# Two-layer encoder with a mixture of experts on one core: query projections and local scores as three single-pass products, heads paired by key group, outputs split straight from PSUM, and an exit by quarters

## The reference, cut to what matters

```
h = RMSNorm(x);  z = h @ W_in -> c_q 384 | c_kv 256 | k_rope 32 | q_B 512 | k_B 128 | v_B 128 | g_A 1024 | g_B 1024
latent attention:  q = rms(c_q) @ W_uq (8 heads, 64 + 32 rotary), k, v from rms(c_kv) @ W_ukv and k_rope
                   softmax over all 256 keys, scale 96 ** -0.5
local attention:   8 heads of 64, 2 key heads (4 query heads each), |q - k| <= 128, relative bias, sink logit per head
x = x + (sigmoid(g_A) * (o_A @ W_oA) + sigmoid(g_B) * (o_B @ W_oB)) @ W_out
x = x + mixture of experts (32 experts, 2 per token) of RMSNorm(x)
```

## Time and profile before

| | |
|---|---|
| median of 3 runs | 1303.14 us |
| the profiled execution | 1301.5 us |
| its span | 1299.7 us |
| PE busy | 1245.8 us (96%) |
| DVE, ACT, POOL busy | 546.8, 415.2, 232.7 us |
| the chain of work that ended last | PE 88%, DVE 4%, DMA 3%, ACT 2% |
| granted TensorE clock, mean | 0.986 |

### The profile page before, as it was taken

How to read it: one execution, slowest core, us unless ns; L and a number is a source line. 1 busy time by engine, 2 the same in 40 slices (tenths; PEclk the granted TensorE clock), 3 DMA queues, 4 the chain that set the end, 5 groups by cost and what they waited for, 6 DMA issues and landing times.

```text
span 1299.7 us, 15960 instructions
## 1 busy us (share of the span) xinstructions
PE 1245.8 (96%) x5860; PEld 814.2 (63%) x5860; DVE 546.8 (42%) x837; ACT 415.2 (32%) x808; POOL 232.7 (18%) x246
## 2 busy tenths in 40 slices
PE   4999999999999999999999999899999899999996
PEld 4976567888874444444588666688888634444443
DVE  4447653342452233333463565434342513333335
ACT  4426663221222222222252467422221222222223
POOL 1343640000102111100324446100010111111000
PEclk9999999999998999999999999999999899999999
DMA  9503003334437999999913300133351599999991
GB/s 298 179 21 97 1 1 118 92 97 146 162 153 287 421 418 419 420 420 423 354 27 112 84 15 1 65 97 98 98 223 54 199 391 420 420 418 420 419 409 73
DMA packets 110521, 278.46 MB, mean 214 GB/s; under 512 B 12240, under 2 KB 74192, under 8 KB 102256
## 3 DMA queue, kind: packets, MB, share of 16 engines
q1 hardware_dynamic: 102752, 259.01, 52.2%
q0 software_dynamic: 6400, 13.74, 3.1%
q10 hardware_dynamic: 1296, 4.72, 0.9%
HBM read 279.52 MB, written 8.40 MB: 222 GB/s over the span
## 4 chain that ended last, share of the span: by engine, by line
PE 88%; DVE 4%; DMA 3%; ACT 2%; DVEq 1%; ACTq 1%; issue 1%; POOL 0%; SPq 0%
PE bank L1197 82%; PE bank L1463 2%; DMA ring<-w_gate_up 2%; PE bank L1332 2%; ACT arena L789 1%; DMA ring<-w_in 1%; DVE arena L873 1%; PE bank L1212 1%; DVE small L1023 1%; PE bank L1510 1%; ACTq L792 1%; PE bank L1395 0%; DVE small L1021 0%; PE bank L1257 0%; DVEq L1022 0%
## 5 line engine op out<-in xcount | busy, mean ns | idle before, releaser
L1197 PE MATMUL bank<-arena 128*64 128x512 f32 (+4 forms) x1410 | 319.2, 518 | 4.7 <-ACTq L755 1.9
L1197 PEld LDWEIGHTS bank<-arena 128*64 128x64 f32 (+2 forms) x1410 | 140.9, 151 | 157.2 <-issue 132.7
L1197 PE MATMUL bank<-ring,arena 128*64 128x512 f32 (+1 forms) x800 | 187.2, 599 | 0.8 <-DMA ring<-w_gate_up 0.4
L1197 PE MATMUL bank<-y_parts,chosen 128*128 128x512 f32 x512 | 134.0, 405 | 0.2
L1197 PEld LDWEIGHTS bank<-ring,arena 128*64 128x64 f32 (+1 forms) x800 | 59.9, 140 | 113.9 <-issue 112.3
L1143 DVE TENSOR_TENSOR x<-x,bank 128x512 f32<-128x512 f32 x128 | 88.0, 687 | 59.0 <-PE bank L1197 58.8
L1197 PEld LDWEIGHTS bank<-y_parts,chosen 128*128 128x128 f32 x512 | 91.2, 188 | 22.7 <-issue 3.5
L1197 PE MATMUL bank<-hT_gate_low,w_chunk_high 128*128 128x512 f32 x256 | 101.4, 396 | 2.1 <-DVE hT_gate_low L1037 2.1
L1197 PE MATMUL bank<-hT_gate_high,w_chunk_low 128*128 128x512 f32 x256 | 101.1, 395 | 0.0
L1197 PE MATMUL bank<-hT_gate_high,w_chunk_high 128*128 128x512 f32 x256 | 101.1, 395 | 0.0
L1164 DVE TENSOR_TENSOR arena<-arena,bank 128x256 f32<-128x256 f32 x32 | 13.5, 421 | 203.6 <-ACT arena L841 203.6
(11 more groups left out here) (205 smaller groups left out, 1917.2 us busy)
## 6 DMA issues: line engine op xcount, KB each, us to landing
ring<-w_gate_up SPq DMA_DIRECT2D x32, 2048.0 KB, 17.7
arena<-w_gate_up SPq DMA_DIRECT2D x32, 2048.0 KB, 18.2
ring<-w_down SPq DMA_DIRECT2D x32, 1024.0 KB, 16.8
arena<-w_down SPq DMA_DIRECT2D x32, 1024.0 KB, 17.8
ring<-w_in SPq DMA_DIRECT2D x36, 512.0 KB, 6.1
arena<-w_out SPq DMA_DIRECT2D x8, 1024.0 KB, 6.3
ring<-w_in SPq DMA_DIRECT2D x4, 1024.0 KB, 12.7
ring<-w_oa SPq DMA_DIRECT2D x16, 256.0 KB, 2.9
```

The costliest lines, as they stand in the source:

```text
L1197: return pe.matmul(out, lhsT, rhs, start=first, stop=last)
```

## The change

- **Queries:** `wq` and c_q (after the transposes) get a high and a low part; each query projection is `mm3` over three chunks. POOL builds `wk` first, then `wq` high (the same 24 instructions), then `wq` low: 12 subtractions and 12 small instructions more. c_q high is an ACT copy, c_q low a DVE subtraction out of PSUM. The parts take the place in the ring of column block 1's weights, so SP loads that block only after the last projection.
- **Local scores:** z tiles 8 to 12 are split by ACT (high) and DVE (low). The host permutes the head columns so that the pair in one tile has one head of each key group; a head's scores then take 64 rows of q and of k, as `mm3`, and `kz` with its zero halves goes.
- **Softmax:** the scale 96 ** -0.5 moves into the query copies and the rotary table; the maximum is written negated; the sink goes into its column by a maximum over one element, issued before the wait for the scores.
- **Outputs:** latent pairs get one rounded ACT copy; DVE subtracts straight from PSUM, in iterations 12, 14 and 16 and once after the loop, and the next output waits for it. hT_gate goes by quarters in the order of `GATE_K`. The first merge starts with the local half and waits for the last low part only before its last chunk.
- **cT** is made in the order 3, 4, 5, 0, 1, 2 in other banks.

The core of the diff:

```
-    rope_rows = np.concatenate([rows, rows], 1).astype(np.float32)
+    rope_rows = np.concatenate([rows, rows], 1).astype(np.float32) * np.float32(MLA_SCALE)
...
+        GATE_K = (6, 0, 2, 4)
+        LOW_AT = {4: 3, 5: 6, 6: 7}
...
# SP
+                    if j == 1:
+                        sp.wait_ge(proj_ps, l * 12 + 12)
+                        sp.nop(nofuse=True)
# POOL: kz fills removed; wk built here, before wq
+                    src, high, low_ = raw[:, :, e::2, :], wq_parts[0][:, :, e::2, :], wq_parts[1][:, :, e::2, :]
...
+                    pool.drain()
+                    for k in range(3):
+                        pool.tensor_tensor(low_[:, k, :, r0:r0 + 32], src[:, k, :, 64:96], high[:, k, :, r0:r0 + 32], ALU.subtract)
+                        pool.tensor_tensor(low_[:, k, :, n0:n0 + 64], src[:, k, :, 0:64], high[:, k, :, n0:n0 + 64], ALU.subtract)
+                    pool.drain()
+                    for k in range(3):
+                        pool.tensor_scalar(low_[:, k, :, r0 + 32:r0 + 48], low_[:, k, :, r0 + 16:r0 + 32], -1.0, None, ALU.mult)
+                        pool.tensor_copy(low_[:, k, :, r0 + 48:r0 + 64], low_[:, k, :, r0:r0 + 16])
# ACT
+                    if t >= 8:
+                        act.activation(z_split(t)[0], z_bank(t)[:, :], ACT.Copy).then_inc(z_high, 1)
+                        continue
...
+                act.wait_ge(cT_ps, l * 6 + 2)
+                act.activation(cT[:, 4, :], cT_bank(4)[:, :], ACT.Copy).then_inc(cT_act, 1)
+                for t in range(3):
+                    act.wait_ge(cT_ps, l * 6 + 4 + t)
+                    act.activation(cq_parts[0][:, t, :], cT_bank(t)[:, :], ACT.Copy).then_inc(cT_act, 1)
...
-                        act.activation(oT[:, 1 - m // 4, m % 4, :], bank[6][:, :], ACT.Copy)
-                        if m >= 4:
-                            act.activation(oT_high[0][m - 4], bank[6][:, :], ACT.Copy)
-                        act.drain().then_inc(oT_done, 1)
+                        act.activation(oT[:, 1, m, :] if m < 4 else oT_high[0][m - 4], bank[6][:, :], ACT.Copy).then_inc(oT_done, 1)
# DVE
+                    if t >= 8:
+                        dve.wait_ge(z_high, l * NZ_SPLIT + t - 7)
+                        dve.tensor_tensor(z_split(t)[1], z_bank(t)[:, :], z_split(t)[0], ALU.subtract).then_inc(z_low, 1)
...
+                for t in range(3):
+                    dve.wait_ge(cT_act, l * 4 + 2 + t)
+                    dve.tensor_tensor(cq_parts[1][:, t, :], cT_bank(t)[:, :], cq_parts[0][:, t, :], ALU.subtract).then_inc(cT_dve, 1)
...
+                        if n < H:
+                            dve.tensor_reduce(soft[:, n % 2, :, S:S + 1].rearrange("p c o -> p (c o)"),
+                                              sink_b[:, n:n + 1].unsqueeze(1).broadcast_to([P, C, 1]), AX.X, ALU.max)
+                        dve.wait_ge(scores_ps, l * HEADS + n + 1)
...
-                            dve.tensor_copy(soft[:, n % 2, :, S:S + 1].rearrange("p c o -> p (c o)"), sink_b[:, n:n + 1].broadcast_to([P, C]))
                             dve.drain()
-                            step(dve.tensor_reduce(mx, soft[:, n % 2, :, :], AX.X, ALU.max))
-                            dve.tensor_scalar(negmax[:, n % 2, :], mx, -1.0, None, ALU.mult).then_inc(negmax_ready, 1)
+                            dve.tensor_reduce(negmax[:, n % 2, :], soft[:, n % 2, :, :], AX.X, ALU.max, negate=True).then_inc(negmax_ready, 1)
...
-                            dve.drain()
-                            dve.tensor_scalar(negmax[:, n % 2, :], mx, -MLA_SCALE, None, ALU.mult).then_inc(negmax_ready, 1)
+                            peak.then_inc(negmax_ready, 1)
...
+                    for i in {HEADS - 2: (0,), HEADS - 1: (1,), HEADS: (2, 3)}.get(n, ()):
+                        dve.wait_ge(hT_gate_high, l * 4 + i + 1)
+                        dve.wait_ge(proj_ps, l * 12 + (12 if i else 10))
+                        k = slice(GATE_K[i], GATE_K[i] + 2)
                         dve.tensor_tensor(hT_gate[1][:, k, :], hT[:, k, :], hT_gate[0][:, k, :], ALU.subtract).then_inc(hT_gate_low, 1)
+                    if n in (12, 14, 16):
+                        low_output(n // 2 - 2)
+                low_output(7)
# PE
+                    if t == NZ_K:
+                        pe.wait_ge(z_low, l * NZ_SPLIT + 1)
+                for t in CT_ORDER:
+                    if t == 0:
+                        pe.wait_ge(z_low, l * NZ_SPLIT + 4)
...
+                pe.wait_ge(z_low, l * NZ_SPLIT + NZ_SPLIT)
...
-                            m = mm(bank[7][:, :], wq[:, k, 2 * j + kind - 1, :], cT[:, k, :], k == 0, k == 2)
+                            m = mm3(bank[7][:, :], [w[:, k, 2 * j + kind - 1, :] for w in wq_parts], [c[:, k, :] for c in cq_parts], k == 0, k == 2)
...
-                        if m_ >= 1:
+                        if 1 <= m_ <= 4:
                             pe.wait_ge(oT_done, l * H + m_)
+                        if m_ >= 5:
+                            pe.wait_ge(oT_low_ready, l * H + LOW_AT[m_ - 1])
...
+                                    rows = slice(n % 2 * HD, (n % 2 + 1) * HD)
+                                    q = qB_high[rows, n // 2, q0:q0 + P], qB_low[n // 2][rows, q0:q0 + P]
+                                    m = mm3(out, q, [k_[rows, b * S:(b + 1) * S] for k_ in kB], True, True)
...
-                        pe.wait_ge(oT_low_ready, l * H + H)
-                    for m in range(2):
+                        pe.wait_ge(oT_low_ready, l * H + H - 1)
+                    for m in (1, 0):
                         for k in range(4):
                             i = 4 * m + k
+                            if (j, m, k) == (0, 0, 3):
+                                pe.wait_ge(oT_low_ready, l * H + H)
```

More of the change, by code:

```diff
@@ L158, in encoder_kernel @@
         qBT_, qBT_at = take(4 * T)
-        kz_, _ = take(4 * T)
+        kz_, kz_at = take(4 * T)
         vB_, vB_at = take(C * P)
@@ L584, in _ @@
                 pool.nop(nofuse=True)
+                pool.wait_ge(ukv_in, l * 16 + 16)
+                pool.nop(nofuse=True)
+                raw_k = ukv_raw.rearrange("p k (h n) -> p k h n", h=H)
+                for k in range(2):
+                    pool.tensor_copy(wk[:, k, :].rearrange("p (h n) -> p h n", h=H), raw_k[:, k, :, 0:NOPE])
+                pool.drain().then_inc(wk_built, 1)
                 for e in range(2):
-                    src, dst = raw[:, :, e::2, :], wq[:, :, e::2, :]
+                    src, high, low_ = raw[:, :, e::2, :], wq_parts[0][:, :, e::2, :], wq_parts[1][:, :, e::2, :]
@@ L595, in _ @@
[L595 to L600, removed]
+                        pool.tensor_copy(high[:, k, :, n0:n0 + 64], src[:, k, :, 0:64])
+                        pool.tensor_copy(high[:, k, :, r0:r0 + 32], src[:, k, :, 64:96])
@@ L692, in _ @@
                 high_part(in_parts[1], in_in[1], l * 16 + 16)
-                for t in range(0, NZ, 2):
+                for t in (0, 2, 4, 6, 8, 9, 10, 11, NZ_K):
                     act.wait_ge(z_ps, l * NZ + t + 1)
[L696 to L700, removed]
+                    if t >= 8:
+                        act.activation(z_split(t)[0], z_bank(t)[:, :], ACT.Copy).then_inc(z_high, 1)
                         continue
@@ L789, in _ @@
                                 e = act.activation(soft[:, n % 2, c, 0:S], bank[2 * (n % 2) + i][:, b * S:(b + 1) * S],
-                                                   ACT.Exp, bias=negmax[:, n % 2, c:c + 1], scale=MLA_SCALE,
+                                                   ACT.Exp, bias=negmax[:, n % 2, c:c + 1], scale=1.0,
                                                    accum_out=rowsum[:, n % 4, c:c + 1])
@@ L1265, in value_rows @@
                 def value_rows(c):
+                    if c >= 1:
+                        pe.wait_ge(cT_dve, l * 5 + 2 + c)
                     for k in range(2):
@@ L1291, in gate_product @@
                     w = chunk_parts[j % 2]
-                    for k in range(KD):
-                        if j == 0 and m == 0 and k % 4 == 0:
-                            pe.wait_ge(hT_gate_low, l * 2 + 1 + k // 4)
-                        i = 8 + m * KD + k
-                        mm3(bank[4 * (j % 2) + 2 + m][:, :], (w.high[:, i, :], w.low[:, i, :]), [h[:, k, :] for h in hT_gate], k == 0, k == KD - 1)
+                    for at, k0 in enumerate(GATE_K):
+                        if j == 0 and m == 0:
+                            pe.wait_ge(hT_gate_low, l * 4 + at + 1)
+                        for k in (k0, k0 + 1):
+                            i = 8 + m * KD + k
+                            mm3(bank[4 * (j % 2) + 2 + m][:, :], (w.high[:, i, :], w.low[:, i, :]), [h[:, k, :] for h in hT_gate],
+                                k == GATE_K[0], k == GATE_K[-1] + 1)
                 for n in range(HEADS + 3):
@@ L1568 @@
     arrays = {n: np.ascontiguousarray(inputs[n]) for n in _INS}
+    pairs = [h // 2 + 4 * (h % 2) for h in range(H)]
```

(4 more changed lines are left out.)

112 lines of the change are left out of this document (43 added, 69 removed).

## The result

The changed kernel takes 1293.83 us (median of 4 runs, 1292.76 to 1296.91), the kernel before 1302.72 in the same measurements: ratio 0.9933, 95% interval 0.9918 to 0.9949. Forecast were 1288 and a gain of 14.9; measured is a gain of 8.9. Direction, place and most sizes of the forecast hold; two things are missing from it, one inside the local heads and one of the clock.

The account below looks back on a forecast made before the run. In the local half PE and the DVE-ACT lap were taken as almost equal limits, with time mostly PE's own work. Per layer -2.1 + 4.7 + 4.1 + 0.75 = 7.45, 14.9 in all, gave 1288 us, range 1279 to 1298.

Parts of the forecast that it names:

- Head 0 late behind POOL, -2.1: Before head 0's transposes: PE waits for the normalisation queued behind POOL's weight splitting, a loss of 2.1 us a layer.
- Local half, +4.7: Heads 0 to 6: PE's work falls from 36.57 to 31.9 us and PE sets the pace, 4.7 us a layer won.
- 12 x 0.118 = 1.42: Local scores of a head: 12 single passes 0.118 us apart take 1.42 instead of 1.73, 2.5 a layer saved.
- the second rival: Local scores: weight loads don't hide under 256 columns, pace 0.234, 22 us lost, 1310 us; chance 0.06.
- laps near 5.7: Sign in the local half that the new sink maximum waits for POOL's port as the old copy did.
- Queries, 3.8 a layer: Query projections: three single passes replace each float32 product, 0.47 us a query, 8 queries, 3.8 us of PE a layer.
- Latent half, +4.1: Head 6 to the gates: four queries' work (1.9) and shorter PE waits win 4.1 us a layer.
- Exit, +0.75: Before the merge: PE's wait shrinks until the split of column block 1 is late next, 0.75 us a layer won.
- Clock, 0 between -3 and +1.5: TensorE's clock: a shorter exit wait may give back 1.5 us, head 0's new wait may take it; net 0.
- POOL's price (1): Rival: POOL's queue ends later than 100.7, each microsecond costing one a layer; 1298 at 105.5, 1309 at 111; chance 0.12.
- the port (3): Rival: the sink maximum waits as the copy did, lap 5.65 us, 2 us a layer lost, 1292; chance 0.10.
- hT_gate's quarters (4): Rival: quarters in iterations 14 and 15 wait beside POOL's normalisations, 2.7 us a layer lost, 1293; chance 0.08.

Follow-up runs that it names:

- low part later: Changed kernel with POOL's low part of the odd heads' wq moved behind the normalisations of heads 1 and 2: 1287.20 us, ratio 0.9879.
- padded keys: Changed kernel with local keys padded with zeros to 128 rows, one tile for each head parity: 1286.72 us, ratio 0.9871.
- plain local scores: Changed kernel with local scores alone as plain float32 products again, on keys padded to 128 rows: 1290.31 us, ratio 0.9893.
- plain queries: Changed kernel with query projections as plain float32 products again, no low part of wq on POOL: 1292.82 us, ratio 0.9926.
- old sink: Changed kernel with keys padded to 128 rows and wq's odd-head low part later on POOL, plus DVE's sink copy again: 1292.47 us, ratio 0.9921.

## Why the prediction was right or wrong

- **Head 0 late behind POOL, -2.1: right.** POOL's work took 18.5 us (82.86 to 101.32), 18.4 in the forecast. PE waited 2.12; its stretch grew by 2.38. The low part later removes it.
- **Local half, +4.7: the step that failed.** Not its limits: PE sets it, DVE's lap (4.89) lies below. The term "12 x 0.118 = 1.42" counted the pace inside a run and left out its two ends: the second rival's mechanism (loads not hidden) exists, but only where the tile changes, here between 64 and 128 rows, 0.39 a head with its query. Six heads, 2.25 a layer, 4.5 in all: the padded keys give back just that and land on 31.71. With it the local scores' saving on 64 rows is zero, as plain local scores confirm. The trace before held the price at its changes of columns: 0.52 instead of 0.43 from a query to an output (above), and transposes of 0.93 behind the outputs' 64-column tiles (148.81 to 149.74) and 0.87 behind 128x128 ones. The sign "laps near 5.7" came true (33.96 / 6 = 5.66), but by PE's work and not by the port that it was meant for.
- **Queries, 3.8 a layer: 3.4 measured.** In PE's work they give 0.50 each, not 0.47 (plain queries take 1.99 more in either half); part of it is waited away again in the latent half.
- **Latent half, +4.1: 4.90.** Idle fell by 2.39 (4.63 to 2.24), 2.2 forecast, with head 15's wait growing by 0.31 as forecast; busy fell by 2.51 (44.79 to 42.28), 0.6 more than forecast, and 0.5 of it stays with plain queries too (44.27). By the starts of the same products these are five intervals, 0.05 to 0.16 longer in the kernel before, which the modelled ends count as busy (the largest: 8 score records from 154.91 take 1.89 instead of 1.73, the idle time behind them left out).
- **Exit, +0.75: 0.97.** Column block 1's split is the next limit, as forecast: PE waits 0.18 for it at 202.86.
- **Clock, 0 between -3 and +1.5: both effects came true together, the loss beyond its bound.** The exit gave back 1.5, by the one profile of the kernel before; the wait at head 0 cost 4.0 on average and up to 8.0.
- Sum: 2 x 6.10 + 1.5 - 4.0 = 9.7 against 8.9 measured, inside the interval of the ratio (6.6 to 10.7). Between the two first profiles the spans differ by 5.7 only: 8.9 from this stage (12.2 + 1.5 - 4.8), less 3.2 in the rest of the program. Its two long parts (between the layers' stretches, and behind them) differ by 3.5 and 4.8 between the profiles of all the kernels here, so 3.2 is within chance; no run takes it apart.
- Luck: part of the misses cancel, which helps the time to lie inside its range. Over both layers the local half lacks 4.2, head 0 0.6 and the clock 2.5; the latent half and the exit give 2.0 more than forecast.
- Rivals: POOL's price (1) was within 0.6; the port (3) did not hold the sink maximum (0.16 inside a normalisation); hT_gate's quarters (4) took 1.2 each inside the loop and only the last two were stretched (4.04 for both, beside the last normalisation): over the 1.5 that was named as the sign, but off the path, since the first 24 gate products took 5.66 as before.

## What to carry to other kernels

Price a run of small products by its ends as well as by its pace: if the products beside it use another tile, in rows or in columns, add the loads that nothing covers, and zero rows can be cheaper than a change of tile. Work added to a shared queue "that is idle" is paid where the next customer of that queue stands; move it behind that customer, when its own user is later. And a wait of 2 us on PE may cost more than its length, by the clock of what follows.

## What the runs showed of the hardware

The Trainium skill, "TensorE: Matmul & The Clock Gate", section "The mechanism", has a weight load overlap a running product when the row group differs or when it goes to the background buffer. The traces don't bear out the first as a condition: within one row group loads of 0.18 to 0.19 us start under the running product and hide, at products 0.119 apart. Which buffer a load takes, no run here shows.

A load is uncovered where the tile changes: between 128 and 64 rows, and also between 128 and 64 columns on the same rows (0.32 instead of 0.233). The price is about 0.1 us for each of the up to four neighbouring intervals.

Every fall of the clock seen from head 0 to the first merge stood behind a PE wait of 1.95 to 2.35 us (2.1 and 2.35 at head 0, 1.95 at head 7 with the old sink, 2.05 at the exit before), and not behind each of them. Behind the four waits of 1.8 with padded keys none was seen.
